# The memory keys of heads 0 and 1 of the second layer: from the expert stage of the first to its own mixing

## The reference, cut to what matters

```
h = rms_norm(x, mix_norm_g[l]);  proj = h @ w_in[l]          # u, v, q, k, vv
gm = gmlp_group(gelu(u), gelu(v), ...);  at = gqa_group(q, k, vv, ...)
x = x + concat([rms_norm(gm), rms_norm(at)]) @ w_out[l]       # the mixing
x = x + memory_cross_attention(rms_norm(x), mem_n, xattn_w_q[l], xattn_w_kv[l], xattn_w_o[l])
x = x + expert_choice_moe(rms_norm(x), w_router[l], w_gate[l], w_up[l], w_down[l])   # 16 experts
```

## Time and profile before

| | |
|---|---|
| median of 3 runs | 2158.29 us (2156.76 to 2159.55) |
| the profiled execution | 2155.34 us, its span 2153.5 us |
| TensorE busy | 1902.0 us, 88% of the span |
| VectorE, ScalarE busy | 909.3 us (42%), 698.3 us (32%) |
| moved by DMA | 592.53 MB, mean 275 GB/s |
| chain that ended last | TensorE 63%, DMA 28%, VectorE 3%, ScalarE 2% |

### The profile page before, as it was taken

How to read it: one execution, slowest core, us unless ns; L and a number is a source line. 1 busy time by engine, 2 the same in 40 slices (tenths; PEclk the granted TensorE clock), 3 DMA queues, 4 the chain that set the end, 5 groups by cost and what they waited for, 6 DMA issues and landing times.

```text
span 2153.5 us, 37456 instructions
## 1 busy us (share of the span) xinstructions
PE 1902.0 (88%) x16680; PEld 1283.3 (60%) x16680; DVE 909.3 (42%) x1337; ACT 698.3 (32%) x1019; POOL 48.2 (2%) x68
## 2 busy tenths in 40 slices
PE   9999968888868999866776689999999999999998
PEld 7898324332224785312222248677999896779996
DVE  6445211000104754101110138458677475486774
ACT  5544100000003643211111135325544443255443
POOL 2000000000000100000000000000000000000000
PEclk9999989999989999988888899999999999999999
DMA  9365999999999367999999995032853360238540
GB/s 339 131 241 222 408 423 423 428 423 423 428 428 394 126 239 329 428 428 428 428 428 428 428 399 191 4 113 97 273 196 137 115 235 4 89 110 275 182 161 20
DMA packets 142207, 592.53 MB, mean 275 GB/s; under 512 B 5840, under 2 KB 59296, under 8 KB 116720
## 3 DMA queue, kind: packets, MB, share of 16 engines
q1 hardware_dynamic: 140960, 586.68, 68.9%
q0 software_dynamic: 1104, 3.70, 0.5%
HBM read 589.30 MB, written 1.05 MB: 274 GB/s over the span
## 4 chain that ended last, share of the span: by engine, by line
PE 63%; DMA 28%; DVE 3%; ACT 2%; SPq 1%; issue 1%; DVEq 0%; POOL 0%; POOLq 0%; ACTq 0%
PE ps L654 36%; DMA ring<-in_w_up 20%; PE ps L1634 8%; DMA ring<-in_w_down 7%; PE ps L3149 3%; PE ps L1668 1%; PE ps L3198 1%; PE ps L1678 1%; PE ps L671 1%; SPq L886 1%; PE ps L1072 1%; DVE ring_lo L630 1%; DMA ring<-in_w_in 1%; ACT slab_hi L625 1%; PE ps L3296 1%
## 5 line engine op out<-in xcount | busy, mean ns | idle before, releaser
L1634 PE MATMUL ps<-ring,area 128*32 128x512 f32 x1728 | 276.9, 691 | 152.7 <-DMA ring<-in_w_up 152.7
L630 DVE TENSOR_TENSOR ring_lo<-ring,slab_hi 128x2048 fp32r<-128x2048 f32 (+2 forms) x137 | 302.8, 2213 | 179.1 <-ACT slab_hi L625 178.9
L625 ACT ACTIVATE slab_hi<-ring 128x2048 fp32r<-128x2048 f32 (+2 forms) x137 | 253.3, 1851 | 252.9 <-PE ps L654 235.9
L1634 PEld LDWEIGHTS ps<-ring,area 128*32 128x32 f32 x1728 | 65.5, 125 | 322.6 <-DMA ring<-in_w_up 183.7
L654 PE MATMUL ps<-hT_hi,slab_hi 128*128 128x256 f32 x832 | 234.4, 282 | 0.5 <-DVE ring_lo L630 0.5
L654 PE MATMUL ps<-hT_hi,ring_lo 128*128 128x256 f32 x832 | 232.7, 280 | 0.0
L654 PE MATMUL ps<-hT_lo,slab_hi 128*128 128x256 f32 x832 | 232.4, 279 | 0.0
L2006 ACT ACTIVATE area<-ps 128x512 f32<-128x512 f32 x32 | 19.1, 597 | 547.5 <-PE ps L1634 507.1
L2643 DVE COPY area<-ps 128x256 f32<-128x256 f32 x32 | 13.6, 424 | 411.4 <-PE ps L1539 411.4
L1668 PE MATMUL ps<-ring,area 128*32 128x512 f32 x984 | 121.2, 610 | 53.7 <-DVE area L2674 31.0
L654 PEld LDWEIGHTS ps<-hT_hi,slab_hi 128*128 128x128 f32 x832 | 156.5, 188 | 1.3 <-DVE ring_lo L630 1.1
(11 more groups left out here) (493 smaller groups left out, 3264.1 us busy)
## 6 DMA issues: line engine op xcount, KB each, us to landing
ring<-in_w_down SPq DMA_DIRECT2D x59, 2048.0 KB, 25.6
ring<-in_w_up SPq DMA_DIRECT2D x58, 2048.0 KB, 21.1
ring<-in_w_gate SPq DMA_DIRECT2D x56, 2048.0 KB, 15.5
ring<-in_w_ffn_up SPq DMA_DIRECT2D x44, 1024.0 KB, 8.2
ring<-in_w_in SPq DMA_DIRECT2D x18, 2048.0 KB, 12.8
ring<-in_w_ffn_down SPq DMA_DIRECT2D x10, 2048.0 KB, 7.8
area<-in_w_gate SPq DMA_DIRECT2D x6, 2048.0 KB, 12.9
ring<-in_xattn_w_kv SPq DMA_DIRECT2D x4, 2048.0 KB, 17.8
```

Of the source, the lines that this page charges most:

```text
L625: return m.nc.scalar.activation(hi, whole, ACT.Copy)
L630: return m.nc.vector.tensor_tensor(lo, whole, hi, ALU.subtract)
L1634: ins = mm(ps[32 * g:32 * g + CAP, 1, :], m.tokT[:, k, :], rows[:, (g % 2) * BANK:(g % 2 + 1) * BANK], start=k == 0, stop=k == KD - 1)
```

## The change

The keys of heads 0 and 1 of the second layer (columns 0 to 511 of `xattn_w_kv[1]`) are no longer made in jobs. Six jobs are left, two for keys (heads 2 and 3) and four for values, and three slabs instead of four. The 2 MB of weights of the two heads are loaded as two transfers of 1 MB, four k-rows each, into the empty second halves of the slots of the first two `w_out` halves (`key_rows`); their slots' landing counts grow from 16 to 32. On TensorE `first_keys(b, i)` makes one 128-column part of the keys from both slots: eight f32 products. It is called four times, between `attended(0)` and `attended(1)`. VectorE copies the two banks out. `second_up(0)` is issued behind `w_xq` and waits for these products, which still read the memory's columns. The diff, cut to its core:

```
-        self.plan, self.landed, self.held = ring_plan([(s, 1) for s in slots])
+        self.plan, self.landed, self.held = ring_plan([(s, 1 if memory or i not in (4, 5) else 2) for i, s in enumerate(slots)])
-JOBS = 8
-MEMORY_JOB_SIGNALS = ("xk", "xk", "xk", "xk", "xv0", "xv0", "xv1", "xv2")
+JOBS = 6
+MEMORY_JOB_SIGNALS = ("xk", "xk", "xv0", "xv0", "xv1", "xv2")
+def key_rows(m, slot):
+    return m.ring[:, slot, SLAB // 2:].rearrange("p (k n) -> p k n", n=BANK)
...
     for j in range(4):
         half(DENSE[l].w_out + j, d["w_out"], *OUT_ORDER[l][j])
+        if l and j < 2:
+            slot = DENSE[l].plan[DENSE[l].w_out + j].slot
+            sp.dma_start(key_rows(m, slot), layer(d["xattn_w_kv"])[:, 4 * j:4 * j + 4, 0:BANK]).then_inc(m.landed[slot], 16)
...
-    else:
-        sp.wait_ge(*m.at("xv2_full", l))
-        second_up(0)
     for j in range(2):
         whole(DENSE[l].w_xq + j, d["xattn_w_q"], j * BANK, BANK)
...
+    if l:
+        sp.wait_ge(*m.at("xka_full", l))
+        second_up(0)
     for j in range(2):
         whole(DENSE[l].w_xo + j, d["xattn_w_o"], j * BANK, BANK)
...
+LATER_XK_BANKS = (5, 4)
+    def first_keys(b, i):
+        for j in range(2):
+            landed1(m, pe, l, DENSE[l].w_out + j)
+            w = key_rows(m, DENSE[l].plan[DENSE[l].w_out + j].slot)
+            for k in range(4):
+                ins = mm(ps[:, LATER_XK_BANKS[b], i * T:(i + 1) * T], w[:, k, (2 * b + i) * P:(2 * b + i + 1) * P], m.memT[:, 4 * j + k, :],
+                         start=j == 0 and k == 0, stop=j == 1 and k == 3)
+        if i == 1:
+            ins.then_inc(m.s("xka_full"), 1)
...
         attended(0)
+        first_keys(0, 0)
+        first_keys(0, 1)
+        pe.wait_ge(*at("at_rows", l, 1))
+        first_keys(1, 0)
         probability_columns(1)
         pe.wait_ge(*at("bg_xn", l))
         pe_columns(m, m.xn, m.s("bg_T"), range(2), bank=6)
+        first_keys(1, 1)
         attended(1)
-        pe.wait_ge(*at("at_rows", l, 1))
+        pe.wait_ge(*at("xka_cols", l))
         out_of_branches(0)
...
+        def first_keys(b):
+            dve.wait_ge(*at("xka_full", l, b + 1))
+            v.tensor_copy(m.xkT[1][:, 2 * b:2 * b + 2, :], two(ps[:, LATER_XK_BANKS[b], :])).then_inc(s("xka_cols"), 1)
+        first_keys(0)
         branch_rows(0, "bg")
         probability_columns(1)
         dve_low_columns(m, dve, m.hT_lo, m.hT_hi1, m.par1("branch_g"), *at("bg_cols_a", l, 0), s("bg_cols_d"), range(2), bank=6)
+        first_keys(1)
         attended(1)
```

More of the change, by code:

```diff
@@ L258, in group @@
     GROUPS[name] = (pre, *layers, mid, *[second] * L, post)
-group("mem", pre=[("mem_loaded", 16 * NT)], first=[("memory_weights_loaded", 64)], later=[], mid=[("down_rows_loaded", 16)])
+group("mem", pre=[("mem_loaded", 16 * NT)], first=[("memory_weights_loaded", 48)], later=[], mid=[("down_rows_loaded", 16)])
 group("ident", pre=[("ident_loaded", 16)])
@@ L349 @@
              ("xoa1_hi", 1), ("xpTb_a", 1), ("xob_hi", 2)])
-group("memk_pe", first=[("xk_full", 4), ("xv0_full", 2), ("xv1_full", 1), ("xv2_full", 1)])
+group("memk_pe", first=[("xk_full", 4), ("xv0_full", 2), ("xv1_full", 1), ("xv2_full", 1)],
+      later=[("xk_full", 2), ("xv0_full", 2), ("xv1_full", 1), ("xv2_full", 1), ("xka_full", 2)])
 group("memk_act", first=[("xk_cols", 3), ("xv0_rows", 2), ("xv1_rows", 1), ("xv2_rows", 1)],
-      later=[("xk_cols", 4), ("xv0_rows", 2), ("xv1_rows", 1), ("xv2_rows", 1)])
-group("memk_dve", first=[("xk0_cols", 1)], later=[])
+      later=[("xk_cols", 2), ("xv0_rows", 2), ("xv1_rows", 1), ("xv2_rows", 1)])
+group("memk_dve", first=[("xk0_cols", 1)], later=[("xka_cols", 2)])
 group("mem_scale", first=[("xs_scale", 1)])
@@ L949, in memory_weights @@
         else:
-            sp.wait_ge(*m.at("xk_full" if j < 3 else "xv0_full", 1, (1, 3, 1)[j - 1]))
-        sp.dma_start(m.memory_weights[j % 2], d["xattn_w_kv"][1].rearrange("(k p) n -> p k n", p=P)[:, :, j * BANK:(j + 1) * BANK])\
+            sp.wait_ge(*m.at(("xk_full", "xv0_full")[j - 1], 1, 1))
+        sp.dma_start(m.memory_weights[j % 2], d["xattn_w_kv"][1].rearrange("(k p) n -> p k n", p=P)[:, :, (j + 1) * BANK:(j + 2) * BANK])\
             .then_inc(m.s("memory_weights_loaded"), 16)
@@ L1477, in memory_job_read @@
     name = MEMORY_JOB_SIGNALS[j]
-    return m.at("xk_cols", 1, j + 1) if j < 4 else m.at(name + "_rows", 1, j - 3 if name == "xv0" else 1)
+    return m.at("xk_cols", 1, j + 1) if j < 2 else m.at(name + "_rows", 1, j - 1 if name == "xv0" else 1)
 def tensor_experts(m, pe, l, release, free_released, next_columns):
@@ L1724, in memory_job @@
         w = m.memory_weights[j // 2 % 2]
-        if j < 4:
+        if j < 2:
             for i in range(2):
-                c = (2 * (j % 2) + i) * P
+                c = (2 * j + i) * P
                 for k in range(KD):
@@ L2014, in memory_job @@
         name = MEMORY_JOB_SIGNALS[j]
-        if j < 4:
+        if j < 2:
             act.wait_ge(*at("xk_full", 1, j + 1))
-            go(m.xkT[1][:, 2 * j:2 * j + 2, :], two(ps[:, 0, :]), ACT.Copy).then_inc(s("xk_cols"), 1)
+            go(m.xkT[1][:, 4 + 2 * j:6 + 2 * j, :], two(ps[:, 0, :]), ACT.Copy).then_inc(s("xk_cols"), 1)
         else:
-            act.wait_ge(*at(name + "_full", 1, j - 3 if name == "xv0" else 1))
-            half = (j - 4) // 2
+            act.wait_ge(*at(name + "_full", 1, j - 1 if name == "xv0" else 1))
+            half = (j - 2) // 2
             go(m.xv[1][:, j % 2, half * BANK:(half + 1) * BANK], ps[:, 0, :], ACT.Copy).then_inc(s(name + "_rows"), 1)
```

## The result

| | before | changed |
|---|---|---|
| median (20 runs each) | 2156.17 us (2150.68 to 2160.64) | 2160.55 us (2156.69 to 2163.11) |
| profiled execution, its span | 2155.34, 2153.5 us | 2160.79, 2159.0 us |
| TensorE busy | 1902.0 us | 1904.7 us |

The ratio is 1.0019, with an interval of 1.0013 to 1.0024: 4.1 us slower, 2.8 to 5.2. The median of before over 20 runs is 2.1 us lower than the median of three that the prediction started from. The forecast was +3.6 us, which the interval holds. The changed kernel's lines are numbered up to 33 higher: L1204 is L1214, L1192 is L1202, L1668 and L1678 are L1694 and L1704, and the new products are L1253.

What follows compares the result with a forecast made beforehand. The prediction took layer 0's experts as DMA bound and the mixing behind as TensorE bound: -5.5 us for the slab and +9.1 for the products give +3.6, on 2158.29 a forecast of 2161.9 us, range 2158.0 to 2166.0 for 8 in 10.

Steps and rivals of the forecast that it cites:

- Which stage is bound by what: Layer 0's experts are bound by DMA, so TensorE work there is worth nothing; the mixing behind is bound by TensorE.
- The saving, 5.5: Layer 0's experts: one 2 MB slab fewer starts the second layer 5.5 us earlier, bounds 4.9 to 5.7.
- The 4.8 that the prediction set against its sum: Layer 0's slab priced from the Trainium skill, bytes over 436 GB/s whatever the rows; the change would end 0.7 us higher.
- The growth, 9.1: Layer 1's mixing, `attended(0)` to `attended(1)`: 13.82 us of new products lengthen the stretch from 10.96 to 20.06 us.
- The cover, 4.72: Loose time between `attended(0)` and `attended(1)`, waiting for exponentials plus the lower clock behind it, both recovered by the new order.
- The price of a fall, 1.7: One fall of TensorE's granted clock, in the mixing or at a stage's tail, was taken to cost 1.7 us.
- The forecast's place, 2161.9: Whole kernel: +3.6 us on 2158.29, the median of three runs of before; the forecast kept 0.66.
- Transfers and waits at nothing: Mixing: two new key slabs cost nothing (bound 0 to 1 us), the moved `second_up(0)` nothing, every added wait is met.
- The clock falls elsewhere (fourth rival): Second layer's experts or a stage's tail: one clock fall met or missed, 1.7 us, giving 2160.2; chance 0.09.
- Absorbed in layer 1's experts (2152.8): Second rival: layer 1's DMA bound expert stage swallows the 9.1 us growth, leaving -5.5; chance 0.05.
- No gain from the slab (2167.4): Third rival: waiting takes the slab's place in layer 0's experts, stage ends where it did, +9.1 us; chance 0.05.
- No cover (2166.6): First rival, mixing: nothing covered, growth 13.8 us; with just one clock fall 2163.6; chance 0.15 for the rival.

Runs made afterwards that it cites:

- one slab out: Kernel before with one of the four job slabs left out, all eight TensorE jobs kept: 2149.79 us, ratio 0.9971 against before.
- products behind: Changed kernel with the four `first_keys` calls and the two copies moved behind `attended(1)`: 2164.84 us, ratio 1.0041 against before.
- wide rows: Kernel before with all eight jobs and four slabs, each loaded in 4 KB rows instead of 2 KB: 2155.27 us, ratio 0.9997 against before.
- no products: Changed kernel with all but two of the new key products left out, transfers, waits and copies kept: 2149.56 us, ratio 0.9977 against before.

## Why the prediction was right

- **Which stage is bound by what.** Right. A slab taken out of layer 0's experts is worth 4.1 to 8.6 us, two jobs of TensorE taken out there nothing that can be seen, and 9 us of TensorE in the mixing arrive whole at the gates and at the end.
- **The saving, 5.5.** The issue of the last `w_down` moved by 5.4 in the profiled pair, and by 3.8 with the second trace of the changed kernel; by runs the saving is 6.3 (4.1 to 8.6). No run's time tells the price by the 2 KB row (5.6) from the one by the bytes (4.9). The rates of the slices put a slab at 5.3 to 5.4, and so nearer to the row: a slab does lower the rate while it passes. The 373 GB/s behind the 5.6 also holds the end of that burst, 347 GB/s from 694 to 700; from 682 to 694 it is 387, by which 2 MB take 5.4. The 4.8 that the prediction set against its sum is therefore too low here; the section that it takes this from has transfers that GpSimd issues, and these slabs are issued by SP.
- **The growth, 9.1.** 9.15 in the profiled pair, and 20.11 or 20.12 us of stretch in all three traces with this order. The count of the products was the step that mattered: 32 in the code, x64 in the trace, 13.8 us. Read as 6.9 the sum would have come out at -3.3.
- **The cover, 4.72.** Right as a sum for the profiled execution: 4.8 us by the moved calls. Its second part, the lower clock behind the pause, was not a fixed part of before. It stands in three traces (before, one slab out, products behind) and is missing in two, one with the same pause (wide rows) and one with a pause of 1.43 us (no products). Without it the stretch is 9.97 instead of 11, so of the 4.72 us about 3.7 are waiting, which goes in either case, and 1.0 is the clock; against an execution without the fall the growth is 10.1 and not 9.1. What the sum took for a cost that the change recovers is there in some executions only, and that the profiled one of before had it was luck of the draw. This makes the change dearer by up to 1 us. The measured +4.1 is 0.5 above the sum, which would fit, but its interval (2.8 to 5.2) is too wide to show it.
- **The price of a fall, 1.7.** The first and fourth rivals took half of the 3.5 us at the lower clock. Measured, a fall is 1.0 us in the stretch and 1.0 to 2.3 us in the tail of the stage.
- **The forecast's place, 2161.9.** It started from a median of before that was 2.1 us too high, and the difference came out 0.5 us above the sum. The two errors partly cancel, so that 2160.55 lies near it is in part luck; the +3.6 is the better test.
- **Transfers and waits at nothing.** Right: no pause of TensorE before the first call, `second_up` 11 us ahead of `w_xo`'s slots, and a tail of 81.1 to 81.2 us in three traces that load the new slabs, as in before without them.
- **The clock falls elsewhere (fourth rival).** They moved, but for the profiled pair upwards: the tail of layer 0 took 1.2 us more, and the span grew by 5.5 us where the sum has 3.6. In the nine traces both positions occur.
- **The rivals.** Absorbed in layer 1's experts (2152.8): out, by the kernel without products. No gain from the slab (2167.4): out, by the slab taken from before. No cover (2166.6): out; it is what the moved calls measure.

## What to carry to other kernels

Price work by the stage in which it lies: here 2 MB in a DMA bound stage were worth 5 to 6 us and 32 f32 products there nothing, and in the stage that received them the reverse held. Work moved into a stage that its engine bounds is free only up to the pauses that it fills, here about 10 of 32 products; put the calls where the pause is, which was worth 4.8 us of 13.8. A fall of the clock that one profile shows may be missing in the next, so it should not be booked as a fixed cost that a change recovers. Before multiplying a count from the code with a duration from the trace, check on one known call how many records a product leaves.

## What the runs showed of the hardware

The same code with the same pause of TensorE (1.66 us) kept its granted clock at 1.00 in one trace (wide rows) and fell to about 0.5, the 1.2 GHz level, for some 3.5 us in two others (before, one slab out); in this stretch that costs 1.0 us (9.97 against 10.96 and 11.06). Another such place is the tail of an expert stage, 81.1 to 81.2 us at a clock of 1.00, or 82.2 to 83.3 with a fall. The fall in one place does not go with that in the other: each of the four combinations stands in a trace. How much of the 10 us between the fastest and the slowest of 20 runs of before comes from this is not shown; the two traces of the changed kernel are already 1.6 us apart ahead of the tail. What decides whether a fall comes is not shown either. The traces fit what the Trainium skill says (page "TensorE: Matmul & The Clock Gate", section "What's actually happening"), that the watch of the clock runs free of the kernel, but none of them shows this watch.

Slabs with rows of 2 KB lower the rate of a queue that is busy throughout: 400 to 410 GB/s in a slice of 9.25 us with a slab, about 427 in the others. Each f32 product of this kernel leaves two records in the trace (16 products, x32), and each transpose one (16 transposes, x16).
